# Recurrence's lane: preparation steps two points apart, masked products sent chunk by chunk, zero state's products left out

## What is computed

```python
def _rwkv7_scan(r, w, k, v, a_vec, b_vec):
    def step(S, inp):
        r_t, w_t, k_t, v_t, a_t, b_t = inp
        sa = jnp.einsum('bhij,bhj->bhi', S, a_t)
        S = S * w_t[:, :, None, :] + sa[..., None] * b_t[:, :, None, :] + v_t[..., None] * k_t[:, :, None, :]
        return S, jnp.einsum('bhij,bhj->bhi', S, r_t)
    S0 = jnp.zeros((Bsz, H, N, N), jnp.float32)
...
def _hgrn2_chunkwise(q, log_f, k, i):
    def step(S, inp):
...
        S = S * jnp.exp(b_last)[..., None] + jnp.einsum('bshd,bshv->bhdv', k_dec, i_c)
        return S, o_intra + o_inter
    S0 = jnp.zeros((Bsz, H, DK, DV), jnp.float32)
```

## Time and profile before

| what | value |
|---|---|
| median of 3 runs | 3349.3 us (3348.35 to 3352.67) |
| profiled execution | 3348.68 us, of which the span is 3346.9 |
| TensorE busy | 3114.3 us, 93% of the span, 15538 matmuls |
| VectorE busy | 1665.1 us, 50% |
| ScalarE busy | 1183.4 us, 35% |
| GpSimd busy | 210.8 us, 6% |
| mean granted TensorE clock | 0.972 |

### The profile page before, as it was taken

How to read it: one execution, slowest core, us unless ns; L and a number is a source line. 1 busy time by engine, 2 the same in 40 slices (tenths; PEclk the granted TensorE clock), 3 DMA queues, 4 the chain that set the end, 5 groups by cost and what they waited for, 6 DMA issues and landing times.

```text
span 3346.9 us, 39218 instructions
## 1 busy us (share of the span) xinstructions
PE 3114.3 (93%) x15538; PEld 2488.4 (74%) x15538; DVE 1665.1 (50%) x2785; ACT 1183.4 (35%) x2056; POOL 210.8 (6%) x421
## 2 busy tenths in 40 slices
PE   7999999999999999999999989998898989888796
PEld 5777777777778877777788767877777776767685
DVE  5444444444433346555633545564655656454545
ACT  4333333333333334434422324343433343343311
POOL 0000000000000000000000020110202020101200
PEclk9999999999999999999999999999999999998898
DMA  4222222222233322222143221221212122121532
GB/s 153 76 76 76 76 76 78 77 79 76 76 107 132 107 76 70 64 72 68 57 162 120 96 70 64 71 83 52 87 55 77 63 71 71 58 71 52 195 126 88
DMA packets 82867, 284.70 MB, mean 85 GB/s; under 512 B 10480, under 2 KB 11120, under 8 KB 81920
## 3 DMA queue, kind: packets, MB, share of 16 engines
q1 hardware_dynamic: 63936, 232.13, 21.5%
q0 software_dynamic: 18752, 50.08, 4.7%
HBM read 256.93 MB, written 25.17 MB: 84 GB/s over the span
## 4 chain that ended last, share of the span: by engine, by line
PE 78%; DVE 10%; DMA 4%; POOL 3%; ACT 3%; issue 3%; SPq 0%; DVEq 0%; ACTq 0%; POOLq 0%
PE bank L257 13%; PE bank L259 12%; PE bank L258 12%; PE bank L261 7%; PE bank L263 7%; PE bank L262 7%; PE bank L281 2%; POOL mc L1783 2%; PE bank L433 1%; POOL mc L1780 1%; PE bank L1248 1%; PE bank L1184 1%; PE bank L1189 1%; DMA mats<-mc 1%; PE bank L310 1%
## 5 line engine op out<-in xcount | busy, mean ns | idle before, releaser
L257 PE MATMUL bank<-ma_split,mc_split 128*128 128x512 f32 x2304 | 963.1, 418 | 38.9 <-DVE ma_split L809 18.6
L674 DVE TENSOR_TENSOR mc_split<-mc,mc_split 128x1024 fp32r<-128x1024 f32 x426 | 522.0, 1226 | 863.8 <-ACT mc_split L523 861.1
L259 PE MATMUL bank<-ma_split,mc_split 128*128 128x512 f32 x2304 | 909.7, 395 | 0.0
L258 PE MATMUL bank<-ma_split,mc_split 128*128 128x512 f32 x2304 | 907.0, 394 | 0.0
L523 ACT ACTIVATE mc_split<-mc 128x1024 fp32r<-128x1024 f32 x426 | 451.2, 1059 | 873.9 <-PE bank L257 471.5
L257 PEld LDWEIGHTS bank<-ma_split,mc_split 128*128 128x128 f32 x2304 | 439.6, 191 | 155.5 <-issue 60.9
L259 PEld LDWEIGHTS bank<-ma_split,mc_split 128*128 128x128 f32 x2304 | 437.4, 190 | 97.6
L258 PEld LDWEIGHTS bank<-ma_split,mc_split 128*128 128x128 f32 x2304 | 440.1, 191 | 78.3 <-issue 4.1
L261 PE MATMUL bank<-mc_split,ma_split 128*128 128x512 f32 x576 | 231.1, 401 | 3.9 <-DMA ma_split<-y 3.7
L263 PE MATMUL bank<-mc_split,ma_split 128*128 128x512 f32 x576 | 226.4, 393 | 0.0
L262 PE MATMUL bank<-mc_split,ma_split 128*128 128x512 f32 x576 | 226.2, 393 | 0.0
(11 more groups left out here) (361 smaller groups left out, 3724.6 us busy)
## 6 DMA issues: line engine op xcount, KB each, us to landing
mc<-in_w SPq DMA_DIRECT2D x426, 512.0 KB, 3.5
x<-mc POOLq DMA_DIRECT2D x8, 1024.0 KB, 5.3
y<-mb_split POOLq DMA_DIRECT2D x28, 256.0 KB, 2.6
ma_split<-y POOLq DMA_DIRECT2D x28, 256.0 KB, 7.8
mb<-in_xt SPq DMA_DIRECT2D x8, 512.0 KB, 12.2
mc<-in_x POOLq DMA_DIRECT2D x4, 1024.0 KB, 6.0
mc<-x POOLq DMA_DIRECT2D x4, 1024.0 KB, 7.8
mats<-mc POOLq DMA_DIRECT2D x8, 512.0 KB, 5.3
```

The lines of the kernel that those rows point to most:

```text
L257: mm = pe.matmul(banks[j][:], wh[:, c], act_hi[:, kt, :], start=(kt == 0), stop=False)
L258: pe.matmul(banks[j][:], wl[:, c], act_hi[:, kt, :], start=False, stop=False)
L259: last = pe.matmul(banks[j][:], wh[:, c], act_lo[:, kt, :], start=False, stop=(kt == KT - 1))
L674: dve.tensor_tensor(w_low[:, s % NR, :, :], w_raw[:, s % NR, :, :], w_high[:, s % NH, :, :].bitcast(F32), ALU.subtract).then_inc(w_lo, 1)
```

## The change

**Tables.** The first part of the preparation has eight steps two points apart instead of five steps three apart, and begins where it did; the second part begins at 120u + 16 instead of 120u + 18. The reciprocal of 512 columns is made in four pieces of 128, one in each of steps 3 to 6. The masked products stand at 120u + 26, 28, 30 and 32 instead of 28, 31, 34 and 37. The levels begin at 120u + 80 instead of 74 and have steps 2.5 points apart on average instead of 3; the chunk steps begin at 103 instead of 101, the last six steps at 131 instead of 130.

**Sends.** `sub_inverses` stores `m8` chunk by chunk, with four stores each behind its own masked copies, where it was one store behind all. In the sort it is filed under `rw_at(u, CHUNKS)`, the point of the first masked product, 48 points lower than before's 74.

**Left out.** Where the state is zero, its products are left out (RWKV and HGRN, chunk 0), and so is what only makes the last state: per unit and head the 128x128 products number 6 fewer, and 3 transpositions of 12 go, with a few small operations of VectorE.

The diff, cut to its core (what is left out carries the new step numbers through the programs of ScalarE and VectorE, shortens the copies to three chunks, and names other semaphores for the waits on the last state):

```diff
@@ -1011,23 +1011,24 @@
 
             LANE0 = RW0 + 2
             CHUNK_K = 24
-            END = 9 + CHUNK_K
+            PART_B, CHUNKS = 8, 12
+            END = CHUNKS + CHUNK_K
 
             def rw_at(u, k):
 
-                if k < 5:
-                    return (128 * u - 54 if u else 2) + 3 * k
-                if k < 9:
-                    return 120 * u + 18 + 2 * (k - 5)
-                begin = 120 * u + 28
-                i = k - 9
+                i = k - CHUNKS
+                if k < PART_B:
+                    return (128 * u - 54 if u else 2) + 2 * k
+                if k < CHUNKS:
+                    return 120 * u + 16 + 2 * (k - PART_B)
+                begin = 120 * u + 26
                 if i < 4:
-                    return begin + 3 * i
+                    return begin + 2 * i
                 if i < 13:
-                    return begin + 46 + 3 * (i - 4)
+                    return begin + 54 + 5 * (i - 4) // 2
                 if i < CHUNK_K:
-                    return begin + 73 + 5 * (i - 13) // 2
-                return begin + 102 + 3 * (i - CHUNK_K)
+                    return begin + 77 + 5 * (i - 13) // 2
+                return begin + 105 + 3 * (i - CHUNK_K)
 
             def hg_at(h, m):
...
@@ -1079,7 +1080,8 @@
                     if (what, lv) == ("W", LEVELS - 1):
                         CHUNK += [("R0", 6, "act")]
             for c in range(NCH):
-                CHUNK += [(f"R{c}", 6, "act")] * (c > 0) + [(f"U{c}", 4, "dve"), (f"O{c}", 5, "act"), (f"S{c}", 6, "dve")]
+                CHUNK += [(f"R{c}", 6, "act")] * (c > 0) + [(f"U{c}", 4, "dve"), (f"O{c}", 5, "act")]
+                CHUNK += [(f"S{c}", 6, "dve")] * (c < NCH - 1)
             C_BANK = {name: banks[b] for name, b, _ in CHUNK if b}
             C_SEM = {"pe": c_pe, "act": c_act, "dve": c_dve}
...
@@ -1114,8 +1116,8 @@
 
 
 
-            def turn4(pe, bank, x):
-                for t in range(TT):
+            def turn4(pe, bank, x, n=TT):
+                for t in range(n):
                     mm = pe.transpose(bank[:, t * P:(t + 1) * P], x[:, t * P:(t + 1) * P], ident[:])
                 return mm
...
@@ -1206,15 +1208,18 @@
                     else:
                         c_wait(pe, "dve", u, f"T{LEVELS - 1}1")
                     bank = C_BANK[f"O{c}"]
-                    pe.matmul(bank[:, 0:P], ar[:, c, 1, :], stbd, start=True, stop=False)
+                    if c:
+                        pe.matmul(bank[:, 0:P], ar[:, c, 1, :], stbd, start=True, stop=False)
                     for h in range(2):
                         hs = slice(h * HD, (h + 1) * HD)
-                        pe.matmul(bank[:, hs], m8[:, 2 * c + h, P:2 * P], us[:, hs], start=False, stop=False)
-                        mm = pe.matmul(bank[:, hs], m8[:, 2 * c + h, 3 * P:4 * P], vtm[:, c, hs], start=False, stop=(h == 1))
+                        pe.matmul(bank[:, hs], m8[:, 2 * c + h, P:2 * P], us[:, hs], start=(c == 0), stop=False)
+                        mm = pe.matmul(bank[:, hs], m8[:, 2 * c + h, 3 * P:4 * P], vtm[:, c, hs], start=False,
+                                       stop=(c == 0 or h == 1))
                     mm.then_inc(c_pe, 1)
-                    bank = C_BANK[f"S{c}"]
-                    pe.matmul(bank[:, 0:P], btm[:, c, :], us, start=True, stop=False)
-                    pe.matmul(bank[:, 0:P], ktm[:, c, :], vtm[:, c, :], start=False, stop=True).then_inc(c_pe, 1)
+                    if c < NCH - 1:
+                        bank = C_BANK[f"S{c}"]
+                        pe.matmul(bank[:, 0:P], btm[:, c, :], us, start=True, stop=False)
+                        pe.matmul(bank[:, 0:P], ktm[:, c, :], vtm[:, c, :], start=False, stop=True).then_inc(c_pe, 1)
                 else:
                     c = (i - 12) // 3
                     c_wait(pe, "dve", u, f"S{c - 1}")
...
@@ -1222,12 +1227,14 @@
 
             def chunk_r(pe, u, c):
                 if c == 0:
-                    c_wait(pe, "dve", u - 1, f"S{NCH - 1}")
+                    c_wait(pe, "act", u - 1, f"R{NCH - 1}")
                 bank = C_BANK[f"R{c}"]
-                pe.matmul(bank[:, 0:P], ar[:, c, 0, :], stbd, start=True, stop=False)
+                if c:
+                    pe.matmul(bank[:, 0:P], ar[:, c, 0, :], stbd, start=True, stop=False)
                 for h in range(2):
                     hs = slice(h * HD, (h + 1) * HD)
-                    mm = pe.matmul(bank[:, hs], m8[:, 2 * c + h, 2 * P:3 * P], vtm[:, c, hs], start=False, stop=(h == 1))
+                    mm = pe.matmul(bank[:, hs], m8[:, 2 * c + h, 2 * P:3 * P], vtm[:, c, hs], start=(c == 0),
+                                   stop=(c == 0 or h == 1))
                 mm.then_inc(c_pe, 1)
 
             def hg_pe(pe, h, m):
...
@@ -1249,14 +1256,17 @@
                     mm.then_inc(d_done, 1)
                 if m == 17:
                     pe.wait_ge(h_kd, 2 * h + 2)
-                    turn4(pe, D_BANK, hkd).then_inc(d_done, 1)
+                    turn4(pe, D_BANK, hkd, NCH - 1).then_inc(d_done, 1)
                 if 18 <= m < 22:
                     c = m - 18
-                    pe.wait_ge(h_s, 5 * h + c + 1)
-                    pe.matmul(D_BANK[:, 0:P], hqe[:, c * P:(c + 1) * P], hs_, start=True, stop=False)
-                    pe.matmul(D_BANK[:, 0:P], att[:, c, :], hitm[:, c * P:(c + 1) * P], start=False, stop=True)
-                    pe.matmul(D_BANK[:, P:2 * P], hkdtm[:, c * P:(c + 1) * P], hitm[:, c * P:(c + 1) * P],
-                              start=True, stop=True).then_inc(d_done, 1)
+                    pe.wait_ge(h_s, NCH * h + c + 1)
+                    if c:
+                        pe.matmul(D_BANK[:, 0:P], hqe[:, c * P:(c + 1) * P], hs_, start=True, stop=False)
+                    mm = pe.matmul(D_BANK[:, 0:P], att[:, c, :], hitm[:, c * P:(c + 1) * P], start=(c == 0), stop=True)
+                    if c < NCH - 1:
+                        mm = pe.matmul(D_BANK[:, P:2 * P], hkdtm[:, c * P:(c + 1) * P], hitm[:, c * P:(c + 1) * P],
+                                       start=True, stop=True)
+                    mm.then_inc(d_done, 1)
                 if m == 24:
                     pe.wait_ge(h_ready, h + 1)
                     turn4(pe, D_BANK, ho).then_inc(d_done, 1)
...
@@ -1518,15 +1532,19 @@
                 if k == 3:
                     d_out(dve, "rw", u, 2)
                     st(dve.tensor_scalar(sqk, ep, 1e-12, None, ALU.max))
-                    st(dve.reciprocal(sqk, sqk))
+                if 3 <= k < 7:
+
+                    part = slice((k - 3) * P, (k - 2) * P)
+                    st(dve.reciprocal(sqk[:, part], sqk[:, part]))
+                if k == 6:
                     dve.tensor_tensor(kk, kk, sqk, ALU.mult).then_inc(kk_norm, 1)
-                if k == 4:
+                if k == PART_B - 1:
                     d_out(dve, "rw", u, 1)
                     dve.wait_ge(kk_norm, u + 1)
                     st(dve.tensor_scalar(sqk, asg, pc[K_A], omka[:, u:u + 1], ALU.mult, ALU.add))
                     st(dve.tensor_tensor(ksh, ksh, sqk, ALU.mult))
                     dve.scalar_tensor_tensor(sqk, rsh, pc[R_K], ksh, ALU.mult, ALU.mult).then_inc(rkr_ready, 1)
-                if k == 5:
+                if k == PART_B:
                     dve.wait_ge(exps_ready, 4 * u + 4)
                     st(dve.scalar_tensor_tensor(ar[:, :, 0, :], kk.rearrange(chunks, c=NCH), -1.0,
                                                 ea.rearrange(chunks, c=NCH), ALU.mult, ALU.mult))
...
@@ -1763,9 +1783,11 @@
                 mats = lambda x: x.rearrange("(q r) -> q r", q=2 * NCH)[:, 0:CH * CH].rearrange("q (j i) -> j q i", j=CH)
                 blocks = lambda x: x.rearrange("(b r) -> b r", b=2 * NCH * SUBS)[:, 0:SUB * CH].rearrange(
                     "b (j i) -> b j i", i=CH)[:, :, 0:SUB]
-                c_wait(pool, "dve", u, f"G{2 * NCH - 1}")
-                pool.dma_start(mats(a["mats"]), m8[:, :, 0:P]).then_inc(a_out, 16)
-                pool.wait_ge(a_out, 16 * (u + 1))
+                for c in range(NCH):
+                    two_heads = slice(2 * c, 2 * c + 2)
+                    c_wait(pool, "dve", u, f"G{2 * c + 1}")
+                    pool.dma_start(mats(a["mats"])[:, two_heads], m8[:, two_heads, 0:P]).then_inc(a_out, 16)
+                pool.wait_ge(a_out, 16 * NCH * (u + 1))
                 pool.dma_start(ub, blocks(a["mats"])).then_inc(ub_in, 16)
                 if u:
                     pool.wait_ge(yb_out, 16 * u)
...
@@ -1793,7 +1815,7 @@
                 x2_rows = a["x2"].rearrange("(t p) n -> p t n", p=P)
                 ends = sorted([(rw_at(u, RW_K - 1), 0, u) for u in range(UNITS - 1)]
                               + [(hg_at(h, HG_M - 1), 1, h) for h in range(UNITS - 1)]
-                              + [(rw_at(u, 13), 2, u) for u in range(UNITS)])
+                              + [(rw_at(u, CHUNKS), 2, u) for u in range(UNITS)])
```

(18 more changed lines are left out.)

57 lines of the change are left out of this document (31 added, 26 removed).

## The result

The changed kernel takes 3317.5 us (median of 4 executions, 3315.3 to 3319.0), the kernel before beside it on the same chip 3350.7 us (4 executions, 3348.4 to 3352.7). The ratio is 0.9902, with an interval of 0.989 to 0.9914. The profiled execution took 3318.5 us.

A forecast was written before the change was run, and what follows sets the result against it. TensorE's work and idle time were taken as the bound, chiefly first-level waits on GpSimd's inversion chain. Terms -12.7 - 68.5 - 7 + 72 + 5 = -11.2 us, from 3349.3, gave 3338 us; range 3322 to 3364.

The forecast's parts named there:

- left-out products and transpositions: On TensorE, 6 products and 3 transpositions fewer per unit and head, all on its path: 12.7 us gained.
- first level's waits: TensorE's first-level transpositions stop waiting for the load of xt, the chain now being covered: 69.0 us go, less 0.5.
- clock: TensorE's low granted clock behind the first level's waits mostly goes, three new long waits cost some back: net 7 us gained.
- the three stalls, less the usual 0.8 each: VectorE's takes at the ends of hg4, hg5, hg6 wait for stores queued behind GpSimd's inversions: 72 us added.
- spacing and other small waits: Closer level steps and both preparation parts change TensorE's small waits: 5 us added in sum.
- Rival (c): The takes don't wait for the late stores, so the stalls' 72 + 8 us fall away: 3258 us, chance 0.04.
- the length of the stalls: At the three block ends, the 36.8 us inversion-and-store chain less cover by points: stalls of 30.3, 24.8 and 19.0 us.
- rival (d): GpSimd's inversion takes 10.8 us with VectorE at rest, second part neutral: 3330 us; shares the forecast's chance of 0.58.
- Spacing of the steps: Levels 2 us, preparation's first part 4 gained, unit 0's 2 lost, second part 5 (ends 0 and 16): +5 us.
- bounds of 60 to 85 us: The prediction calls itself wrong if the three takes' stalls sum to under 60 or over 85 us.

The follow-up runs named there:

- experiment 3: Changed kernel with as many same-size products and transpositions put back where they had been left out; 3332.5 us, ratio 0.9944.
- experiment 6: Changed kernel with the three heads' stores issued inside the inversions, and levels 37 instead of 48 points behind the masked products; 3310.9 us, ratio 0.9883.
- experiment 1: Changed kernel with sub_inverses sorted in GpSimd's queue at the first level's point again, as before the change; 3260.2 us, ratio 0.973.
- experiment 2: Kernel before the change with only sub_inverses' sort key moved forward to the first masked product; 3401.2 us, ratio 1.015.
- experiment 5: Changed kernel with the stores of heads 3, 4 and 5 issued inside the inversions of units 5, 6 and 7; 3255.9 us, ratio 0.9724.
- experiment 8: Changed kernel with a unit's last six steps one point earlier, putting VectorE's norm ahead of the preparation's five operations; 3321.3 us, ratio 0.9917.
- experiment 9: Kernel of experiment 5 with the last six steps one point earlier and VectorE's multiply out of D_BANK ahead of the five operations; 3244.2 us, ratio 0.9687.
- experiment 10: Changed kernel with the reciprocal of 512 columns in one piece at step 3 instead of four pieces; 3323.2 us, ratio 0.992.
- experiment 4: Changed kernel with one send of m8 behind all masked copies instead of four quarter sends; 3328.2 us, ratio 0.9933.

## Why the prediction was right in sign and wrong in size

Against the sum of -11.2 us, the profiled executions differ by 30.2. By its steps:

| step | forecast | measured | from |
|---|---|---|---|
| left-out products and transpositions | -12.7 | -12.4 to -15.0, work -14.3 | experiment 3 |
| first level's waits | -68.5 | -68.7 | L1181 |
| clock | -7 | -7.6 | work left beside the products, 21.9 - 14.3 |
| the three stalls, less the usual 0.8 each | +72 | +65 | timeline, 67.3 - 2.4 |
| spacing and other small waits | +5 | -3 | idle time that is left |
| ahead of rw1's block | 0 | -1.7 | its first matmul |

**What held.** The first level's waits went as worked out, and experiment 6 shows that 48 points are what does it. The stalls stand at the three boundaries named, shrink downwards from the end of hg4, and come from the sort key (experiments 1 and 2). Rival (c), the takes don't wait, is refuted. Its 3258 us is near what the kernels without stalls measure, 3260.2 and 3255.9, but partly by chance: experiment 1 has 11.8 us of waits at the first level that (c) had at 0.5, and the small waits that shrank make up for them. The clock's term held as well; three 6 us stretches behind the stalls, after (length, then each engine's busy time, granted clock, DMA share, GB/s):

```profile
2648.10:2654.10 6.00, 5.95 (x17) 4.79 (x18) 4.43 (x7) 4.50 (x6) 0.00 (x0) 0.53 0.30 90
2820.60:2826.60 6.00, 5.86 (x20) 4.80 (x21) 4.42 (x7) 4.50 (x6) 0.00 (x0) 0.68 0.30 87
2989.90:2995.90 6.00, 5.93 (x18) 4.81 (x19) 4.42 (x7) 5.02 (x7) 0.00 (x0) 0.57 0.26 87
```

They lie where those behind the waits of L1179 lay, between the levels of 1.2 and 2.4 GHz, however long the wait was. Removing the three takes 9.2 us off the work in experiment 1 (1234.0 against 1243.2) and 7.6 in experiment 5 (1235.6); 8 were forecast.

**The first failed step: the length of the stalls.** 30.3, 24.8 and 19.0 were forecast; 27.1, 23.1 and 17.1 came, 6.8 us less together. For the first, from the last send's issue to TensorE's start:

| piece | forecast | measured |
|---|---|---|
| send to issue of the block load | 2.9 | 2.62 |
| block load to first multiply | 4.1 | 3.36 |
| multiplies and adds | 11.9 | 10.67 |
| to the issue of the last load | 4.0 | 4.04 |
| to head 3's first store | 4.6 | 4.89 |
| both stores landed | 3.3 | 3.21 |
| take and TensorE's start | 0.9 | 0.83 |
| sum | 31.7 | 29.62 |

Another 1.1 us lies ahead of the send. Most of the sum's error is the inversion, 11.9 forecast and 10.7 measured, which I took between the disturbed rows and the undisturbed; rival (d), counted with the forecast, had 10.8. Its 3330 us had 3.3 us less of stalls and a neutral second part, and still lay 12 us too high. The stalls' 7 us taken off the forecast give 3331, so it was not they alone that put the time below 3322.

**The second failed step: "Spacing of the steps", +5 us.** It was worked out one sided, with 0 to 16 as ends and nothing below zero. Its parts went both ways. In the second part the wait behind `D_BANK` grew as described, L1149 from 5.9 to 14.9 us, where the forecast allowed 5 net; the mechanism, the bonus product's bank freed behind the five operations, was named rightly, and experiments 8 and 9 show it. In the chunk steps a wait of 8.1 us behind the state (L1233) is new, and one of 3.6 (L1209) went. But elsewhere more was gained than the 4 us allowed. The turns at L1119 (L1121) waited 11 us less, the 4.7 us behind the sigmoid's copy among them; the steps of the levels no longer wait 3.8 us for VectorE's masked copies; the blocks' first matmuls (L257) outside the three stalls waited some 5 us less. The reciprocal's pieces, which the forecast gave nothing, are worth some 5 us (experiment 10). The sum of all small waits is 3 us less, where 5 more were forecast, and that lies outside the ends of 0 and 16. Only the pieces' part was isolated; how the others divide between the two-point spacing, the levels' new place and the missing operations of VectorE was not tried.

**The price of a product held.** The distance of two neighbours gives 12.7 us; put back in their own places the same products and transpositions cost 12.4 us from rw1 on and 15.0 in the medians. Work and clock together came to 21.9 us where 19.7 were forecast, 2.2 more.

Together: stalls 7.1 (72 less 64.9), small waits 7.8 and work 2.2, 0.2 at the first level and 1.7 ahead of rw1's block are the 19.0 by which the profiled executions miss the sum; another 1.6 lies between these and the medians (the execution before 0.6 below the median that the forecast started from, the one after 1.0 above its own). The two failed steps alone give 3338.1 - 14.9 = 3323, just inside the range. The last 6 us, work and scatter between executions, carried it below 3322. The stalls lie within their bounds of 60 to 85 us; the small waits don't.

## What to carry to other kernels

When a routine with waits in it is moved forward in a queue, list what is queued behind it and who waits for that: here one sort key took back 57 of 90 us, and putting each head's two short stores inside the routine gives them back. When many small steps move, cost the waits that vanish with the same care as those that come; a term with only one sign needs a reason why the other can't be. A wait for an operand may be a wait for the bank it is turned through, and then freeing the bank earlier helps where producing the operand earlier doesn't.

## What the runs showed of the hardware

**GpSimd's pace.** The same 30 multiplies and adds take 10.7 to 11.6 us in units 5 to 7 of the changed kernel and 12.5 to 17.3 in the others. Unit 5's inversion in the changed kernel, then in the kernel of experiment 1 (length, busy time of TensorE, its weight loads, VectorE, ScalarE, GpSimd, clock, DMA share, GB/s):

```profile
2624.51:2635.18 10.67, 0.00 (x0) 0.00 (x0) 0.00 (x0) 0.00 (x0) 8.39 (x30) 0.50 0.00 0
```

```profile
2625.39:2642.18 16.79, 16.79 (x76) 13.91 (x75) 11.12 (x18) 14.01 (x16) 14.52 (x30) 1.00 0.30 95
```

With VectorE busy for 11.12 of 16.79 us the same 30 operations are 14.52 us busy instead of 8.39. Between the operations stand 2.28 us against 2.27, so the difference lies wholly in the operations themselves. These two rows don't tell VectorE from ScalarE and the DMA traffic, which stood at 0 too. The single operations do. Kernel before, unit 2, with the slow operation of the earlier trace rows:

```profile
2254.16 1.06 ACT L523 ACTIVATE mc_split<-mc 128x1024 fp32r<-128x1024 f32 x1 [0.19 <-PE bank L257]
2254.33 0.31 POOL L1783 TENSOR_TENSOR mc<-mc 64x55 f32<-64x55 f32 x1
...
2255.25 1.23 DVE L674 TENSOR_TENSOR mc_split<-mc,mc_split 128x1024 fp32r<-128x1024 f32 x1 [1.57 <-ACT mc_split L523]
2255.47 1.14 POOL L1780 TENSOR_TENSOR mc<-mc 64x39 f32<-64x39 f32 x1
```

In the stall the same two take 0.30 and 0.27 us. I compared all 480 operations of the inversions in the kernel before and in experiment 1 with the same ones in unit 5's stall, summed from the timelines. The 163 with no VectorE instruction beside them take 44.7 us against 44.3, though ScalarE works beside 130 of these, with 60 GB/s of DMA. The 34 beside VectorE instructions that read a PSUM bank take 9.9 against 9.7. The 201 beside VectorE instructions that read both inputs from SBUF take 117.5 against 57.5. So it is these instructions of VectorE that slow GpSimd, and neither ScalarE nor the DMA traffic. The rule of the Trainium skill (GPSIMD Engine Reference, Specifications) that GpSimd's SBUF interfaces are shared with VectorE, with contention where a VectorE instruction has two SBUF inputs, agrees with this.

**Sends.** A quarter of `m8` lands 2.2 us after its issue, the whole in 3.9 (medians, experiment 4): four times the bytes cost 1.7 us more.

**The clock.** In the stall GpSimd works on while the granted clock is 0.50, which is TensorE's lower level; the stretch behind the wait of 17 us is granted 0.57, that behind the one of 27 us 0.53.
